# Order of the work within a weight slot of the attention stage on ScalarE and VectorE of a hybrid decoder layer

## The reference, cut to what matters

```python
x = x + 0.5 * swiglu(rmsnorm(x, ffn1_norm), ffn1_wg, ffn1_wu, ffn1_wd)      # d_ff 5632
h = rmsnorm(x, mix_norm);  proj = h @ w_in                                  # 5680 columns
y_conv = b_gate * conv3(c_gate * c_h)                                       # 1024 channels
# 16 query heads, 4 kv heads of 64: compressed, selected and window branches
s = q @ k.T, masked;  p = softmax(s);  o = sum over branches of gate * (p @ v)
y = concat(rmsnorm(y_conv), rmsnorm(y_attn));  x = x + y @ w_out
x = x + 0.5 * swiglu(rmsnorm(x, ffn2_norm), ffn2_wg, ffn2_wu, ffn2_wd);  rmsnorm(x, final_norm)
```

## Time and profile before

| | us |
|---|---|
| median of 3 runs (lowest, highest) | 1893.97 (1893.65, 1894.42) |
| the profiled execution: its own time | 1894.39 |
| the profiled execution: span in the trace | 1892.6 |
| PE busy in the span | 1865.3 (99%) |
| DVE busy | 1037.6 (55%) |
| ACT busy | 883.1 (47%) |
| POOL busy | 252.7 (13%) |
| mean granted TensorE clock | 0.999 of full speed |

### The profile page before, as it was taken

The page is one execution under the profiler, slowest core; times in us unless marked ns, Lnnn a source line. Parts: engine busy times, 40 slices in busy tenths (PEclk is TensorE's granted clock), DMA queues, the critical chain, the costliest instruction groups (busy, mean ns, idle before and its releaser), DMA issues.

```text
span 1892.6 us, 23078 instructions
## 1 busy us (share of the span) xinstructions
PE 1865.3 (99%) x8387; PEld 1531.8 (81%) x8387; DVE 1037.6 (55%) x1129; ACT 883.1 (47%) x1123; POOL 252.7 (13%) x442
## 2 busy tenths in 40 slices
PE   9999999999999999999998899999999999999998
PEld 7888888888888888888776788888888888888886
DVE  5555555554544444668566766445555555545444
ACT  6444444444444444556555645444444444444443
POOL 1111222111100000000132200111111112200000
PEclk9999999999999999999999999999999999999999
DMA  7666666666655556665433565766666666676564
GB/s 258 209 201 199 200 211 212 210 205 193 213 176 200 200 189 200 195 209 175 146 118 100 171 192 164 220 199 196 210 214 201 204 194 202 211 231 195 194 192 142
DMA packets 199517, 366.72 MB, mean 194 GB/s; under 512 B 19028, under 2 KB 23872, under 8 KB 199328
## 3 DMA queue, kind: packets, MB, share of 16 engines
q1 hardware_dynamic: 185568, 353.41, 59.3%
q0 software_dynamic: 11648, 12.02, 2.2%
q10 hardware_dynamic: 2240, 0.47, 0.1%
HBM read 350.11 MB, written 4.19 MB: 187 GB/s over the span
## 4 chain that ended last, share of the span: by engine, by line
PE 92%; DVE 5%; ACT 3%; issue 1%; ACTq 0%; DVEq 0%
PE ps L586 30%; PE ps L588 30%; PE ps L587 30%; DVE w_lo L1382 2%; PE ps L607 1%; ACT prob L1175 1%; ACT w_hi L977 1%; DVE mins L1627 1%; DVE pT_lo L1633 1%; DVE p_h L1684 0%; PE ps L875 0%; PE ps L636 0%; DVE p_q L1653 0%; PE ps L845 0%; DVE shifted L1650 0%
## 5 line engine op out<-in xcount | busy, mean ns | idle before, releaser
L1382 DVE TENSOR_TENSOR w_lo<-raw,w_hi 128x1024 fp32r<-128x1024 f32 x656 | 798.1, 1229 | 653.3 <-ACT w_hi L977 651.5
L977 ACT ACTIVATE w_hi<-raw 128x1024 fp32r<-128x1024 f32 x656 | 689.8, 1060 | 729.4 <-PE ps L588 720.5
L586 PE MATMUL ps<-w_hi,hT_hi 128*128 128x512 f32 x1760 | 688.0, 391 | 5.2 <-DVE w_lo L1382 5.2
L588 PE MATMUL ps<-w_hi,hT_lo 128*128 128x512 f32 x1760 | 685.4, 389 | 0.0
L587 PE MATMUL ps<-w_lo,hT_hi 128*128 128x512 f32 x1760 | 685.1, 389 | 0.0
L586 PEld LDWEIGHTS ps<-w_hi,hT_hi 128*128 128x128 f32 x1760 | 330.5, 188 | 75.4 <-DVE w_lo L1382 3.9
L588 PEld LDWEIGHTS ps<-w_hi,hT_lo 128*128 128x128 f32 x1760 | 330.3, 188 | 69.5
L587 PEld LDWEIGHTS ps<-w_lo,hT_hi 128*128 128x128 f32 x1760 | 330.5, 188 | 67.6
L528 POOL DMA_DIRECT2D gu_raw<-gu_sq x352 | 187.8, 542 | 854.6 <-DVE gu_sq L1443 778.5
L586 PE MATMUL ps<-w_hi,guT_hi 128*128 128x512 f32 x704 | 274.3, 390 | 0.0
L588 PE MATMUL ps<-w_hi,guT_lo 128*128 128x512 f32 x704 | 274.0, 389 | 0.0
(11 more groups left out here) (212 smaller groups left out, 833.1 us busy)
## 6 DMA issues: line engine op xcount, KB each, us to landing
raw<-in_ffn_wg_dram SPq DMA_DIRECT2D x176, 512.0 KB, 4.4
raw<-in_ffn_wu_dram SPq DMA_DIRECT2D x176, 512.0 KB, 4.7
raw<-in_ffn_wd_dram SPq DMA_DIRECT2D x176, 512.0 KB, 4.0
raw<-in_w_in_dram SPq DMA_DIRECT2D x88, 512.0 KB, 3.6
raw<-in_w_out_dram SPq DMA_DIRECT2D x32, 512.0 KB, 4.7
gu_raw<-gu_sq POOLq DMA_DIRECT2D x352, 32.0 KB, 4.3
x_parked<-x SPq DMA_DIRECT2D x8, 256.0 KB, 5.8
raw<-in_cmp_k_w_dram SPq DMA_DIRECT2D x8, 256.0 KB, 2.9
```

The costliest lines, as they stand in the source:

```text
L586: mm(o, x_hi, w_hi[:, s, kk, :], start=first and kk == 0, stop=False)
L588: ins = mm(o, x_lo, w_hi[:, s, kk, :], start=False, stop=last and kk == GK - 1)
L977: act.activation(w_hi[:, c % SLOTS, :, :], raw[:, c % SLOTS, :, :], ACT.Copy).then_inc(hi_ready, 1)
L1382: tt(w_lo[:, s, :, :], raw[:, s, :, :], w_hi[:, s, :, :].bitcast(F32), ALU.subtract).then_inc(lo_ready, 1)
```

## The change

On ACT, `exps(m)` and `shift_halves` of tick m are put one slot later (`TICK0 + 3 + m`) and ahead of the rest of that slot, and `prob_high(m)` stays at `TICK0 + 2 + m` but is put last in it. So after `prob_high(m)` comes `hi` of the next slot, and then `exps(m)`. On DVE likewise `sum_inverse(m)` and `attended` come one slot later and first, `prob_low(m)` and `score_min(m)` stay and come last: `prob_low(m)`, `score_min(m)`, `lo` of the next slot, `sum_inverse(m)`. Convolution taps and operands move by a slot in part; `projected(KS)` by two slots; some steps around the compression MLP by one (two of them on PE); the RMSNorm statistics at the mixer's and FFN2's start by one or two. No instruction is added or removed.

```diff
@@ PE @@
-                put(at(43), lambda: kT_transposes(0))
-                put(at(48), hid_transposes)
+                put(at(44), lambda: kT_transposes(0))
+                put(at(49), hid_transposes)
@@ ACT, ffn @@
-                    after = {1: [lambda: x_square(RS_FFN2, NDC - 1, 6 * NDC)],
-                             4: [lambda: root(RS_FFN2)], 5: [lambda: x_operand(2, NDC - 1)]}
+                    after = {2: [lambda: x_square(RS_FFN2, NDC - 1, 6 * NDC)], 5: [lambda: x_operand(2, NDC - 1)],
+                             6: [lambda: root(RS_FFN2)]}
@@ ACT, mixer @@
+                for m in range(NT * HEADS):
+                    put(TICK0 + 3 + m, lambda m=m: exps(m))
+                for m in range(TICKS):
+                    if output_at(m) is not None:
+                        put(TICK0 + 3 + m, lambda u=output_at(m): shift_halves(u))
                 for jb in range(N_IN):
                     if jb != CH_LO:
-                        put(done("in", jb) + 1, lambda jb=jb: projected(jb))
+                        put(done("in", jb) + (3 if jb == KS else 1), lambda jb=jb: projected(jb))
-                for m in range(TICKS):
-                    if fill_at(m) is not None:
-                        put(TICK0 + 2 + m, lambda m=m: prob_high(*fill_at(m)))
-                    if m < NT * HEADS:
-                        put(TICK0 + 2 + m, lambda m=m: exps(m))
-                    if output_at(m) is not None:
-                        put(TICK0 + 2 + m, lambda u=output_at(m): shift_halves(u))
...
-                put(o - 2, lambda: conv_operand(2))
-                put(o - 1, lambda: conv_operand(3))
-                put(o, lambda: conv_squares(2))
+                put(o - 1, lambda: conv_operand(2))
+                put(o, lambda: conv_operand(3))
+                put(o + 1, lambda: conv_squares(2))
...
+                for m in range(TICKS):
+                    if fill_at(m) is not None:
+                        put(TICK0 + 2 + m, lambda m=m: prob_high(*fill_at(m)))
@@ DVE, ffn @@
-                             3: [lambda: variance(RS_FFN2, DM, 3 * NDC)],
-                             5: [lambda: x_operand(2, NDC - 1)], 6: [lambda: inverse_root(RS_FFN2)]}
+                             4: [lambda: variance(RS_FFN2, DM, 3 * NDC)],
+                             5: [lambda: x_operand(2, NDC - 1)], 7: [lambda: inverse_root(RS_FFN2)]}
@@ DVE, mixer @@
+                for m in range(NT * HEADS):
+                    put(TICK0 + 3 + m, lambda m=m: sum_inverse(m))
+                for u in range(UNITS - 1):
+                    put(TICK0 + 3 + GRP * u + 9, lambda u=u: attended(u))
...
-                for n, c in enumerate((39, 41, 51, 52)):
+                for n, c in enumerate((42, 43, 51, 52)):
                     put(at(c), lambda n=n: rope_ks(*divmod(n, 2)))
...
-                for n, slots in ((2, (76, 78)), (3, (80, 81)), (0, (88, 89)), (1, (92, 93))):
+                for n, slots in ((2, (77, 78)), (3, (81, 82)), (0, (89, 90)), (1, (93, 94))):
...
+                for m in range(TICKS):
+                    if fill_at(m) is not None:
+                        put(TICK0 + 2 + m, lambda m=m: prob_low(*fill_at(m)))
+                    if m < NT * HEADS:
+                        put(TICK0 + 2 + m, lambda m=m: score_min(m))
```

More of the change, by code:

```diff
@@ L1273, in put @@
                     after.setdefault(c, []).extend(fs)
-                put(MIX0 + 1, lambda: x_square(RS_MIX, NDC - 1, 2 * NDC))
-                put(MIX0 + 4, lambda: root(RS_MIX), gate_w_load)
+                put(MIX0 + 2, lambda: x_square(RS_MIX, NDC - 1, 2 * NDC))
+                put(MIX0 + 4, gate_w_load)
+                put(MIX0 + 6, lambda: root(RS_MIX))
                 put(MIX0 + 5, lambda: x_operand(1, NDC - 1))
+                for m in range(NT * HEADS):
[3 more added lines that the diff above has]
+                        put(TICK0 + 3 + m, lambda u=output_at(m): shift_halves(u))
                 for jb in range(N_IN):
                     if jb != CH_LO:
-                        put(done("in", jb) + 1, lambda jb=jb: projected(jb))
+                        put(done("in", jb) + (3 if jb == KS else 1), lambda jb=jb: projected(jb))
                 at = lambda n: MIX0 + n
@@ L1290, in mixer @@
                     put(at(c), lambda n=n: q_operand(n))
-                for n, c in enumerate((44, 48, 52, 53)):
+                for n, c in enumerate((43, 45, 52, 53)):
                     put(at(c), lambda n=n: q_high(n))
-                put(at(43), gelu_copy)
-                put(at(46), gelu)
-                for n, c in enumerate((45, 47, 55, 56)):
+                put(at(44), gelu_copy)
+                put(at(47), gelu)
+                for n, c in enumerate((46, 48, 55, 56)):
                     put(at(c), lambda n=n: k_high(*divmod(n, 2)))
@@ L1301, in mixer @@
                     put(at(66) + n, lambda n=n: compressed_values(n))
-                for m in range(TICKS):
-                    if fill_at(m) is not None:
-                        put(TICK0 + 2 + m, lambda m=m: prob_high(*fill_at(m)))
-                    if m < NT * HEADS:
-                        put(TICK0 + 2 + m, lambda m=m: exps(m))
-                    if output_at(m) is not None:
-                        put(TICK0 + 2 + m, lambda u=output_at(m): shift_halves(u))
[L1309 to L1313, removed]
+                for m, (kind, n) in EXTRA.items():
+                    if kind == "cu":
+                        put(TICK0 + 3 + m, lambda n=n: u_operand(n))
+                        put(TICK0 + 4 + m, lambda n=n: conv_tap0(n))
                 o = OUT0
-                put(o - 2, lambda: conv_operand(2))
-                put(o - 1, lambda: conv_operand(3))
-                put(o, lambda: conv_squares(2))
+                put(o - 1, lambda: conv_operand(2))
+                put(o, lambda: conv_operand(3))
+                put(o + 1, lambda: conv_squares(2))
                 put(o + 2, lambda: conv_squares(3))
@@ L1804, in mixer @@
                 put(MIX0 + 1, lambda: residual(NDC - 1, MIX0, 1, half))
-                put(MIX0 + 3, lambda: variance(RS_MIX, DM, 2 * NDC))
+                put(MIX0 + 4, lambda: variance(RS_MIX, DM, 2 * NDC))
                 put(MIX0 + 5, lambda: x_operand(1, NDC - 1))
-                put(MIX0 + 6, lambda: inverse_root(RS_MIX))
+                put(MIX0 + 7, lambda: inverse_root(RS_MIX))
+                for m in range(NT * HEADS):
+                    put(TICK0 + 3 + m, lambda m=m: sum_inverse(m))
+                for u in range(UNITS - 1):
+                    put(TICK0 + 3 + GRP * u + 9, lambda u=u: attended(u))
                 at = lambda n: MIX0 + n
@@ L1819, in mixer @@
                 put(at(27), gates_den)
-                for n, c in enumerate((45, 49, 54, 55)):
+                for n, c in enumerate((44, 46, 54, 55)):
                     put(at(c), lambda n=n: q_low(n))
-                for n, c in enumerate((39, 41, 51, 52)):
+                for n, c in enumerate((42, 43, 51, 52)):
                     put(at(c), lambda n=n: rope_ks(*divmod(n, 2)))
-                put(at(44), gelu_cube)
-                for n, c in enumerate((46, 48, 56, 58)):
+                put(at(45), gelu_cube)
+                for n, c in enumerate((47, 49, 56, 58)):
                     put(at(c), lambda n=n: k_low(*divmod(n, 2)))
-                put(at(47), gelu_out)
+                put(at(48), gelu_out)
                 put(at(50), hidden_operand)
@@ L1833, in mixer @@
                 put(at(61), compressed_weigh)
[L1834 to L1841, removed]
                 for t in range(NT):
@@ L1844, in mixer @@
                 put(at(70), conv_pads)
-                for m in range(NT * HEADS):
-                    put(TICK0 + 2 + m, lambda m=m: sum_inverse(m))
-                for n, slots in ((2, (76, 78)), (3, (80, 81)), (0, (88, 89)), (1, (92, 93))):
+                for n, slots in ((2, (77, 78)), (3, (81, 82)), (0, (89, 90)), (1, (93, 94))):
                     for tap in (1, 2):
                         put(at(slots[tap - 1]), lambda n=n, tap=tap: conv_tap(n, tap))
-                put(at(82), conv_input_lower)
+                put(at(83), conv_input_lower)
                 o = OUT0
```

## The result

The changed kernel takes 1872.06 us (median of 4 runs, 1871.49 to 1872.37) against 1894.15 us before (4 runs, 1893.65 to 1894.42): a ratio of 0.9883, 95% interval 0.9866 to 0.9900. Forecast were 1874.4 us and a gain of 19.6.

A forecast was written before the change was run, and what follows sets the result against it. PE's stops, set by a chain of ACT and DVE, were taken as the bound. Idle 17.36 plus 3.0 unseen, less 0.8, gave 19.6 us gained from the profiled 1894.39: 1874.8, or 1874.4 as median; range 1872.8 to 1880.5.

The forecast's parts named there:

- What bounds it: Whole kernel: PE is busy for 1865.3 of 1892.6 us, so only PE's stops can be won.
- The three short loops: Plain tick: loops of ACT 2.4, DVE 2.7 and both 2.8 us, all under PE's 3.76, so PE sets the pace.
- the walk through a unit: Ticks 25 to 29 followed with PE never stopping: 17.4 us, where a unit lasted 20.73.
- the slack: In ticks 25 to 29, prob_low(26) ends 1.2 us before the fill of tick 27 wants its bank.
- The margins for late exponentials and weighing: Ticks: score bank free 4.0 us early in the worst tick; POOL's weighing ends by 14.8, wanted at 17.4.
- the long chain: Rival, chance 0.15: in the ticks, stretched DVE operations delay prob_low, costing 5 us in all, 1879.4 us.
- the late weighing: Rival, chance 0.04: POOL's weighing comes too late, one stop of 1 us in each of six units, 1880.4 us.
- the slower side: Rival, chance 0.04: exps behind hi frees the score bank late, each of 32 ticks paying 0.95 us, 1903 us.
- The edges: Around the ticks and in FFN2: stops of 1.5 us at conv_gate(2), 0.73 near projected(KS) and 0.57 in FFN2 go.
- The thin places: Two or three places with under half a microsecond of margin, including lo(51) and unit 7's weighted values: 0.8 us left.
- The sum: PE's shown idle 17.36 us plus 0.16 for each of 19 stops, 20.4 together; less 0.8, gain 19.6.
- The low end of the range: Whole kernel: 1872.8 us, from all 20.4 us won and 0.7 for the error of counting stops.

The follow-up runs named there:

- pad1: Changed kernel with one unused minimum on DVE ahead of prob_low in slots 84, 88 and 92: 1872.10 us.
- pad2: Changed kernel with two unused minima on DVE ahead of prob_low in slots 84, 88 and 92: 1873.51 us.
- pad4: Changed kernel with four unused minima on DVE ahead of prob_low in slots 84, 88 and 92: 1876.53 us.
- exps_last: Changed kernel with exps(m) a place later on ACT, behind prob_high(m+1): 1879.77 us.
- dve_only: Changed kernel with ACT's order in the ticks put back to that of before, DVE's order as changed: 1906.20 us.
- The three drain runs: Changed kernel with PE waiting for its own last matmul: after each head's scores 1882.38 us, after even heads' 1877.40, after the group in 32 slots 1880.92.
- act_only: Changed kernel with DVE's order in the ticks put back to that of before (remainder last from tick 32 on), ACT's as changed: 1886.43 us.

## Why the prediction was off, point by point

- **What bounds it: right.** All of the gain is PE's stops, and they are gone; ticks 20.0, edges 2.0 us.
- **The three short loops and the walk through a unit: right.** The walk had `prob_low(26)` done 6.3 us after the first fill and the fill of tick 27 at 7.5; the trace has 1009.53 + 0.69 - 1003.71 = 6.5 and 7.52. The unit was to last 17.4 us and lasts 17.38. `pad1`, `pad2` and `pad4` confirm the slack from both sides. The margins for late exponentials and weighing held too (`exps_last`). The rivals of the long chain, the late weighing and the slower side did not occur in the changed kernel; the late weighing did in `dve_only`.
- **The edges: right, with one overlooked.** `conv_gate(2)`, the stop at 845 us and the one in FFN2 are gone, and so is the one at 739.5 us, worth 0.3, which the prediction didn't name. The thin places cost little: `lo` of slot 51 was in time, and the weighted values of unit 7 wait so briefly that it doesn't show as idle of PE, only as 0.34 us for its weight load; their first matmul starts 0.30 us after the one before it (1052.18 - 1051.88) and the second 0.33 after the first, together 0.2 us lost.
- **The sum: here it failed, by size.** The step reads "each of the 19 stops gives 0.16 more: 3.0". From PE's transposes at 562 us to its last matmul the changed kernel is 22.5 us shorter (1884.14 - 562.45 against 1861.30 - 562.13). Of that 17.4 is shown idle, so the unseen part is 5.1 us where the sum has 3.0. The price of a stop was too low: laid beside the changed kernel matmul by matmul, the stops of before cost 0.20 to 0.30 us beyond their shown idle. I had counted only that a matmul's shown time reaches past the start of the next, and not that the matmul after the restart comes 0.1 us late as well, although show it: the matmul behind a stop has 0.50 or 0.51 us, not 0.39. The three drain runs measured the same price apart from everything else: 0.26 behind scores, 0.22 behind a group. The count was low too: there are 22 stops. The waits list leaves out those with under 0.15 us of shown idle, which are the one at 739.5 us and two inside: 0.11 us at 965.53 and 0.14 at 1050.19. At the old price the three are 0.5 of the missing 2.1 us; the higher price of all 22 is the other 1.6.
- **The allowance of 0.8 us for thin places was hardly needed:** only the 0.2 us of unit 7 came, and they are already in the 22.5. So this pair of traces is 2.1 + 0.8 = 2.9 us above the forecast gain. The medians show 2.5, since their difference is 22.1: by chance this pair of executions lies a little further apart. The low end of the range left 0.7 us for an error in counting the stops, where price and count together were wrong by 2.1.
- In the expectations, two mixtures were sized wrong: `act_only` (a stop of 3.4 us where the two engines' places for unit 6 no longer fit) and `dve_only` (its sign: what had run under ACT's `w_hi` came to stand behind it).

## What to carry to other kernels

Where two engines hand work to each other within a slot and both also feed a third, write down the loop that each order leaves: a step that waits for the other engine should have work behind which the wait is spent, on both engines at once; reordering one alone can lose. Follow the busiest stretch by hand from durations of the trace, with the bound engine never stopping: here the slack came out to 0.2 us and the gain followed. And price a stop of PE at its shown idle plus about a quarter of a microsecond: 22 stops of 17.4 us shown were worth 22.5. Count the stops from the starts of the matmuls, since the shortest are in no list of waits.

## What the runs showed of the hardware

**The price of a restart.** 0.28 to 0.33 us for a stop in which PE waits for nothing but its own last matmul, of which 0.06 is shown as idle; 0.33 each with 16 stops behind scores and 0.32 with 32.

**PE's clock after a stop.** In `act_only`, behind the 3.4 us stop, matmuls of 512 columns start 0.43 us apart for a whole group, where it is 0.23 at the full clock, and the granted clock of 1050 to 1060 us is 0.79: the lower of the two levels, 1.2 GHz, for part of the stretch. The same kernel has seven such matmuls behind a stop of 1.86 us at 999.79, with a clock of 0.83 from 1000 to 1010. The second trace of the kernel before has it too, behind a stop of 1.9 us (PE's timeline):

```profile
1004.31 0.91 PE L607 MATMUL ps<-consts,prob 128*128 128x128 f32 x4 [1.86 <-DVE pT_lo L1633]
1004.87 0.78 PE L745 MATMUL ps<-k_hi,q_st 128*128 128x512 f32 x1
...
1007.39 0.63 PE L587 MATMUL ps<-w_lo,hT_hi 128*128 128x512 f32 x1
1007.82 0.47 PE L588 MATMUL ps<-w_hi,hT_lo 128*128 128x512 f32 x1
1008.13 0.39 PE L586 MATMUL ps<-w_hi,hT_hi 128*128 128x512 f32 x1
```

In the first trace of it the same stop (1004.49 on PE) has no such matmuls behind it. PE lost nothing by it: it fell 1.6 us behind the first trace, and by 1016 us, two stops later, had that back, since there it would have stood still anyway. Idle time was turned into slow matmuls, which is why the shown idle of two executions of one kernel differs by 1.5 us. In `act_only` the slow group behind the 3.4 us stop put PE a further 2.2 us behind the changed kernel, and no later stop gave that back: there the clock did cost time. The profiled execution, with a mean clock of 0.996, took 1889.56 us and the other runs, with 0.998, 1886.01 to 1886.74, which fits; only the first has a trace.

**DVE and POOL.** With the inverse behind `w_lo` instead of ahead of it, `lo` takes 1.22 us in each of the ticks 25 to 29, where it took 1.21 to 1.48 before, and POOL is busy for 245.9 us instead of 252.7 for the same work. Before, POOL's weighing ran beside a `w_lo` for 18.1 us in all, by the starts and ends of both; now it is 0.3. It still meets taps: the pair takes 1.10 us at 1002.00, with DVE idle, and 1.51 at 1012.17, beside two taps, which read two tensors in SBUF as `w_lo` does. The Trainium skill (SBUF — State Buffer, Who interferes with whom) says that a VectorE instruction with two SBUF inputs contends with a GpSimd instruction that reads SBUF, and one with at most one SBUF input, outside the two-port modes, does not; these rows fit it, but no run tests it apart.
